# Router logits from unnormalised rows, with the router's transposes and matmuls moved inside the output products

## The reference, cut to what matters

```python
x = x + g1 * y                                  # y = o @ wo, the attention's output product
h2 = _modulate(_rmsnorm(x, norm2_g[i]), sh2, sc2)     # rmsnorm(x) * g * (1 + sc2) + sh2
...
p_grp = softmax((h @ w_r1) + b_r1);  grp = argmax(p_grp)           # h is h2, all tokens
logits2 = einsum('nd,gde->nge', h, w_r2) + b_r2
p_in = softmax(logits2[rows, grp]);  top_p, top_j = lax.top_k(p_in, TOP_K)
...                                             # experts of 1024 -> 2*512 -> 1024, weighted sum
```

## Time and profile before

| what | value |
| --- | --- |
| time, 3 runs | 2983.76 us median (2983.32 to 2985.27) |
| span of the profiled execution, first to last instruction | 2981.8 us |
| median less span | 2.0 us |
| PE busy | 2718.0 us, 91% of the span |
| DVE busy | 1320.2 us, 44% |
| ACT busy | 769.0 us, 26% |
| POOL busy | 607.8 us, 20% |
| mean granted TensorE clock | 0.959 of 2.4 GHz |

### The profile page before, as it was taken

The page is one execution under the profiler, slowest core; times in us unless marked ns, Lnnn a source line. Parts: engine busy times, 40 slices in busy tenths (PEclk is TensorE's granted clock), DMA queues, the critical chain, the costliest instruction groups (busy, mean ns, idle before and its releaser), DMA issues.

```text
span 2981.8 us, 38421 instructions
## 1 busy us (share of the span) xinstructions
PE 2718.0 (91%) x15145; PEld 1490.5 (50%) x15145; DVE 1320.2 (44%) x2419; ACT 769.0 (26%) x1709; POOL 607.8 (20%) x877
## 2 busy tenths in 40 slices
PE   6999999899998996999999969989999869997893
PEld 2444433798897553333333334468884524332331
DVE  3544400799996564111111156479994531110113
ACT  2211100677775101000000034146660100000001
POOL 2555400355554001000000025410000000000000
PEclk9999999999999996999999989989999879999996
DMA  6344468433423227999999864553325479999997
GB/s 251 113 104 141 148 238 280 91 70 77 84 65 116 99 78 299 384 380 426 398 419 396 331 242 141 138 142 65 58 44 205 160 303 417 401 389 397 423 378 291
DMA packets 199410, 684.31 MB, mean 229 GB/s; under 512 B 26688, under 2 KB 122096, under 8 KB 166208
## 3 DMA queue, kind: packets, MB, share of 16 engines
q1 hardware_dynamic: 101344, 583.01, 52.3%
q10 hardware_dynamic: 84896, 61.07, 6.5%
q0 software_dynamic: 12992, 37.77, 3.3%
HBM read 607.81 MB, written 83.43 MB: 232 GB/s over the span
## 4 chain that ended last, share of the span: by engine, by line
PE 78%; DMA 14%; DVE 5%; issue 1%; SPq 1%; ACT 1%; POOL 1%; ACTq 0%; POOLq 0%; DVEq 0%; PEldq 0%
PE psum L461 19%; PE psum L1876 15%; DMA moe_ring<-in_e_w 10%; PE psum L1399 8%; PE psum L1891 8%; PE psum L1048 5%; PE psum L997 5%; PE psum L1186 3%; PE psum L1173 3%; PE psum L1002 2%; PE psum L1214 2%; PE psum L428 1%; PE psum L1388 1%; PE psum L1853 1%; PE psum L2057 1%
## 5 line engine op out<-in xcount | busy, mean ns | idle before, releaser
L1876 PE MATMUL psum<-moe_ring,moe_xT 128*32 128x512 f32 (+2 forms) x3712 | 600.5, 606 | 39.4 <-DMA moe_ring<-in_e_w 37.2
L461 PE MATMUL psum<-qkv_w,act_hT 128*128 128x512 f32 x1376 | 611.8, 598 | 5.5 <-issue 3.1
L461 PEld LDWEIGHTS psum<-qkv_w,act_hT 128*128 128x128 f32 x1376 | 256.4, 191 | 313.3 <-issue 311.2
L1876 PEld LDWEIGHTS psum<-moe_ring,moe_xT 128*32 128x32 f32 (+2 forms) x3712 | 205.7, 123 | 403.2 <-issue 400.4
L1891 PE MATMUL psum<-moe_ring,moe_hT 128*32 128x512 f32 (+2 forms) x1856 | 302.1, 604 | 18.7 <-DMA moe_ring<-in_e_w 17.2
L1960 DVE TENSOR_TENSOR moe_hh<-psum,moe_sg 128x512 f32<-128x512 f32 x42 | 29.0, 691 | 600.0 <-PE psum L1876 600.0
L1399 PE MATMUL psum<-wo,out_oT 128*128 128x512 f32 x576 | 256.1, 599 | 1.9 <-DVEq L1456 1.5
L1928 ACT ACTIVATE moe_sg<-psum 128x512 f32<-128x512 f32 x42 | 25.1, 597 | 749.1 <-PE psum L1876 749.1
L1113 DVE TENSOR_REDUCE att_nmax<-psum 128x1 f32<-128x1280 f32 x144 | 201.8, 1401 | 25.1 <-PE psum L997 23.1
L997 PE MATMUL psum<-att_kT,att_q 128*128 128x512 f32 (+1 forms) x832 | 193.5, 367 | 9.7 <-ACTq L177 5.1
L1065 ACT ACTIVATE att_prob<-psum,att_nmax 128x1280 f32<-128x1280 f32 (+1 forms) x160 | 184.9, 1158 | 48.5 <-DVE att_nmax L1113 45.6
(11 more groups left out here) (263 smaller groups left out, 3294.7 us busy)
## 6 DMA issues: line engine op xcount, KB each, us to landing
moe_ring<-in_e_w SPq DMA_DIRECT2D x192, 2048.0 KB, 20.7
ada_w<-in_ada_w SPq DMA_DIRECT2D x48, 1024.0 KB, 6.5
qk_d<-qkv_stg ACTq DMA_DIRECT2D x112, 256.0 KB, 2.8
att_q<-qk_d SPq DMA_DIRECT2D x32, 640.0 KB, 11.9
att_q<-qk_d SPq DMA_DIRECT2D x64, 256.0 KB, 5.3
qkv_w<-in_a_wqkv SPq DMA_DIRECT2D x6, 2048.0 KB, 10.2
att_kT<-qk_d SPq DMA_DIRECT2D x32, 320.0 KB, 5.7
prep_y<-y_d SPq DMA_DIRECT2D x10, 1024.0 KB, 7.8
```

The source lines that it names most:

```text
L461: ins = nc.tensor.matmul(psum[:, u.par, :], hT[:, k, u.t * P:(u.t + 1) * P], qw[:, u.C % 2, k], start=(k == 0), stop=(k == KD - 1))
L1876: ins = nc.tensor.matmul(psum[part, bank, :], xT[:, 4 * half + k, part], ring[:, slot_of(CHUNK[l][r, half]), k, bank * DE:(bank + 1) * DE] ...
```

## The change

The logits are made from the rows x1 as they are, before the norm. Since h2 = x1 * rs * (gain * (1 + scale)) + shift, with rs one number for a row, the logits are rs * (x1 @ W') + (shift @ W + b), with W' = W whose rows are multiplied by gain * (1 + scale). W' and shift @ W are made once for each layer and each kind of token. For them SP issues three more loads behind the four of the rows, which bring scale, shift and gain as columns: `rcol[p, k]` is element 128k + p, so a load moves 1024 single numbers. That makes six loads in layer 0 and three in layer 1. DVE makes W' and the shifted weights, and PE sums the latter over the partitions with a matrix of ones (`shift_sums`).

The order also changes. PE's transposes of the last tile's x1 stand in the middle of the first half of the product, its `route` behind that half, and `shift_sums` is at that place in the first tile; after the last tile only one `turn` and one `route` are left. DVE does everything for a tile within its own step, and in the last tile makes h2's second operation after the pick. ACT's `lower` waits for h2 before it issues its store. ACT no longer waits for the stores: SP does before expert weights (layer 1) or before its later loads (layer 0), and POOL does before the first gather.

```diff
 def sp_post, step
+                for n, src in enumerate([mod_d[l, t, 4 * D:5 * D], mod_d[l, t, 3 * D:4 * D], norm2_g[l]]):
+                    sp.dma_start(rcol[:, t, n], src.rearrange("(k p) -> p k", p=P), allow_slow_non_contiguous=True).then_inc(s_rcol, 16)
 def pe_post
         def turn(T, par):
-            pe.wait_ge(s_h2, T + 1)
+            pe.wait_ge(s_x1, T + 3)
...
+        def shift_sums():
+            for s in range(2 - l):
+                pe.wait_ge(s_wrs, 2 * l + s + 1)
+                nc.tensor.matmul(psum[:, 6, s * (NG + NE):(s + 1) * (NG + NE)], ones[:, :], wshsum[:, s], start=True, stop=True).then_inc(s_rsh, 1)
...
                 for k in range(KD):
+                    if n == 0 and t and k == KD // 2:
+                        turn(T - 1, 1 - par)
                     ins = nc.tensor.matmul(psum[:, 2 * par + n, :], (oT1 if l else oT)[:, k, t * P:(t + 1) * P], wo[:, k, n * HALF:(n + 1) * HALF], start=(k == 0), stop=(k == KD - 1))
-                if n == 0 and not first:
-                    route(T - 2, par)
+                if n == 0:
+                    if t:
+                        route(t - 1, 1 - par)
+                    else:
+                        shift_sums()
             ins.then_inc(s_y, 1)
-            if not (first and t == 0):
-                turn(T - 1, 1 - par)
...
-        route(T - 2, 0)
         turn(T - 1, 1)
-        route(T - 1, 1)
+        route(TILES[l] - 1, 1)
 def dve_post
+        def router_weights(s):
+            dve.wait_ge(s_rcol, 96 + 48 * l)
+            dvec.link(dve, nc.vector.scalar_tensor_tensor(rcol[:, s, 0], rcol[:, s, 0], 1.0, rcol[:, s, 2], ALU.add, ALU.mult))
+            nc.vector.tensor_tensor(wrs[:, s], wrt[:, l], col_of(0), ALU.mult)
+            dvec.link(dve, nc.vector.tensor_tensor(wsh[:, s], wrt[:, l], col_of(1), ALU.mult))
+            nc.vector.reduce_sum(wshsum[:, s], wsh[:, s].rearrange("p k n -> p n k"), AX).then_inc(s_wrs, 1)
...
+            scaled(T, par, s)
+            if not last:
+                shifted(T, par, s)
+            logit(T, t, par, s)
+            ins = dve_pick(dve, l, t)
+            if last:
+                shifted(T, par, s)
+                ins.then_inc(s_rtp, 1)
...
+        for s in range(2 - l):
+            router_weights(s)
+        for s in range(2 - l):
+            router_bias(s)
+        tile_steps(dve, TILES[l], step)
 def act_post
+            act.wait_ge(s_h2, T + 1)
             act.dma_start(h2_d[ds(t * P, P), :], h2[:, par]).then_inc(s_h2st[par], 16)
...
-        for s in s_x1st + s_h2st:
-            act.wait_ge(s, 16 + 16 * (TA // 2 if l == 0 else (TA + TX) // 2))
 def sp_moe_first (layer 1) and sp_moe (layer 0)
+            for s in s_x1st + s_h2st:
+                sp.wait_ge(s, post_stored(l))
 def pool_moe
+        for s in s_h2st:
+            pool.wait_ge(s, post_stored(l))
```

More of the change, by code:

```diff
@@ L1307, in build @@
     s_bc, s_bcd = [sem("s_bc0"), sem("s_bc1")], sem("s_bcd")
+    s_rcol, s_wrs, s_rsh, s_rbias = sem("s_rcol"), sem("s_wrs"), sem("s_rsh"), sem("s_rbias")
     A = Arena("post")
@@ L1340, in build @@
     bc1 = A("bc1", [P, 1, 4, D])
+    rcol = A("rcol", [P, 2, 3, KD])
+    wrs = A("wrs", [P, 2, KD, NG + NE])
+    wsh = A("wsh", [P, 2, KD, NG + NE])
+    wshsum = A("wshsum", [P, 2, NG + NE])
+    rbias = A("rbias", [P, 2, NG + NE])
     BC, XT = [bc, bc1], [xt, xt1]
@@ L1379, in turn, with route @@
             for k in range(KD):
-                ins = nc.tensor.transpose(psum[:, 4 + k // 4, (k % 4) * P:(k % 4 + 1) * P], h2[:, par, k * P:(k + 1) * P], ident)
+                ins = nc.tensor.transpose(psum[:, 4 + k // 4, (k % 4) * P:(k % 4 + 1) * P], x1[:, par, k * P:(k + 1) * P], ident)
             ins.then_inc(s_h2t, 1)
-        def route(T, par):
+        def shift_sums():
+            for s in range(2 - l):
+                pe.wait_ge(s_wrs, 2 * l + s + 1)
+                nc.tensor.matmul(psum[:, 6, s * (NG + NE):(s + 1) * (NG + NE)], ones[:, :], wshsum[:, s], start=True, stop=True).then_inc(s_rsh, 1)
+        def route(t, par):
+            T = TA * l + t
+            s = int(t >= TX)
             pe.wait_ge(s_h2ta, T + 2)
@@ L1386, in route @@
             pe.wait_ge(s_rld, T + 1)
+            if t == 0:
+                pe.wait_ge(s_rbias, 2 + l)
             for k in range(KD):
-                ins = nc.tensor.matmul(psum[:, 6 + par, 0:NG + NE], h2T[:, par, k, :], wrt[:, l, k, :], start=(k == 0), stop=(k == KD - 1))
+                ins = nc.tensor.matmul(psum[:, 6 + par, 0:NG + NE], h2T[:, par, k, :], wrs[:, s, k, :], start=(k == 0), stop=(k == KD - 1))
             ins.then_inc(s_rl, 1)
@@ L1460, in dve_post, with router_bias @@
             dve_fixed(dve)
+        def router_weights(s):
+            col_of = lambda n: rcol[:, s, n].unsqueeze(2).broadcast_to([P, KD, NG + NE])
+            dve.wait_ge(s_rcol, 96 + 48 * l)
[3 more added lines that the diff above has]
+            nc.vector.reduce_sum(wshsum[:, s], wsh[:, s].rearrange("p k n -> p n k"), AX).then_inc(s_wrs, 1)
+        def router_bias(s):
+            dve.wait_ge(s_rsh, 2 + l)
+            nc.vector.tensor_tensor(rbias[:, s], psum[:, 6, s * (NG + NE):(s + 1) * (NG + NE)], brt[:, l, :], ALU.add).then_inc(s_rbias, 1)
         def upper(T, par):
@@ L1465, in upper, with scaled, shifted, logit @@
             nc.vector.tensor_copy(h2T[:, par, 4:8, :], psum[:, 5, :].rearrange("p (b n) -> p b n", b=4)).then_inc(s_h2td, 1)
-        def logit(t, par):
-            T = TA * l + t
+        def scaled(T, par, s):
+            dve.wait_ge(s_x1rs, T + 1)
+            nc.vector.scalar_tensor_tensor(hm[:, par], x1[:, par], xrs[:, par:par + 1], BC[l][:, s, 2], ALU.mult, ALU.mult).then_inc(s_h, 1)
+        def shifted(T, par, s):
+            dve.wait_ge(s_h, T + 1)
+            dve.wait_ge(s_h2st[par], 8 * (T - par + 2))
+            nc.vector.tensor_tensor(h2[:, par], hm[:, par], BC[l][:, s, 1], ALU.add).then_inc(s_h2, 1)
+        def logit(T, t, par, s):
             dve.wait_ge(s_rl, T + 1)
-            nc.vector.tensor_tensor(logits[:, ds(t, 1), :].rearrange("p o n -> p (o n)"), psum[:, 6 + par, 0:NG + NE], brt[:, l, :], ALU.add).then_inc(s_rld, 1)
+            dve.wait_ge(s_rbias, 2 * l + s + 1)
+            nc.vector.scalar_tensor_tensor(logits[:, t, :], psum[:, 6 + par, 0:NG + NE], xrs[:, par:par + 1], rbias[:, s], ALU.mult, ALU.add).then_inc(s_rld, 1)
+            dve.wait_ge(s_rld, T + 3)
         def step(t, par):
             T = TA * l + t
-            s = int(isinstance(t, int) and t >= TX)
-            begin = isinstance(t, int) and t in (0, TX)
+            s = int(t >= TX)
+            begin = t in (0, TX)
             if begin:
@@ L1487, in step @@
             dve.sem_inc(s_pinfree, 1)
-            later = not (isinstance(t, int) and t == 0)
-            if later:
-                upper(T - 1, 1 - par)
+            upper(T, par)
             if begin:
                 dve.wait_ge(s_bcd, 1 + s + 2 * l)
[L1493 to L1505, removed]
+            last = t == TILES[l] - 1
+            scaled(T, par, s)
[6 more added lines that the diff above has]
+                ins.then_inc(s_rtp, 1)
+            else:
+                dvec.link(dve, ins)
+        for s in range(2 - l):
[3 more added lines that the diff above has]
+        tile_steps(dve, TILES[l], step)
     def act_post(act, l):
@@ L1511, in act_post, with lower @@
             act.sem_inc(s_h2ta, 1)
-        def lower(t, par, whole=False):
+        def lower(t, par):
             T = TA * l + t
@@ L1528, in step @@
             act.dma_start(xs_d[ds(t * P, P), :], x1[:, par]).then_inc(s_x1st[par], 16)
-            if not (isinstance(t, int) and t == 0):
-                lower(t - 1, 1 - par)
+            lower(t, par)
         tile_steps(act, TILES[l], step)
-        lower(TILES[l] - 1, 1, True)
-        for s in s_x1st + s_h2st:
-            act.wait_ge(s, 16 + 16 * (TA // 2 if l == 0 else (TA + TX) // 2))
     def pool_post(pool, l):
@@ L1797, in sp_moe_loads, with post_stored @@
                 sp.dma_start(ring[:, slot_of(n)].rearrange("p k f -> p (k f)"), src.rearrange("p o k f -> p (o k f)")).then_inc(s_ring[slot_of(n)], 16)
+    def post_stored(l):
+        return 16 + 16 * (TA // 2 if l == 0 else (TA + TX) // 2)
     def sp_moe_first(sp, l):
+        if l:
+            for s in s_x1st + s_h2st:
+                sp.wait_ge(s, post_stored(l))
         sp.wait_ge(s_exptab, l + 1)
@@ L1804, in sp_moe @@
     def sp_moe(sp, l):
+        if l == 0:
+            for s in s_x1st + s_h2st:
+                sp.wait_ge(s, post_stored(l))
         sp.wait_ge(s_xg[0], xg_count(l, 0))
```

5 lines of the change are left out of this document (1 added, 4 removed).

## The result

The changed kernel takes 3006.78 us (median of 4 runs, 3004.87 to 3011.47) against 2983.54 for the one before (4 runs, 2977.60 to 2985.27). That is 23.2 us slower, where 3002 us was forecast. The measured ratio is 1.0086, with a 95% interval of 1.0073 to 1.0098; the two medians alone give 1.0078. The profiled execution has a span of 3004.3 us, 22.5 more than before.

What follows compares the result with a forecast made beforehand. PE alone was taken to limit post's loop. 16.9 + 10.0 + 3.4 + 1.0 - 5.0 - 8.2 = +18.1 us on the 2981.8 span, plus 2.0 to the median, gave 3002 us; range 2988 to 3009, eight in ten 2991 to 3017.

Steps and rivals of the forecast that it cites:

- PE's wait: First tile of post: PE idles for the columns before its second half product, clock loss included; +16.9 us layer 0, +10.0 layer 1.
- the clock's share: After PE's idle stretch in the first tile the clock is at half for 5 us; 2.5 us lost in each layer.
- Why the columns are late: Start of post: column loads queue behind the rows on SP, 0.7 us each, six 4.2, landing at 974.5 in layer 0.
- One of its signs of being wrong: Column loads in post: the prediction is wrong if one takes more than 1.5 us of the queue.
- 2.0 us for each transfer: Column loads: if each paid about 2.0 us in turn, six would be 12 us and the sum rise by about 11.7.
- Rival 1: Column loads of single numbers cost 2.7 us each in the queue; nine at 2.0 more make +18, 3020 us; chance 0.15.
- Rival 2: PE's turns inside the products wait for x1; half a us for each of 16 is +8, 3010 us; chance 0.05.
- Rival 3: Columns pass the rows at post's start, PE idles 4.3 and about 1.1 us; -0.9, 2983 us, no change; chance 0.08.
- Rival 4: PE doesn't wait for the columns at all in the first tile; -8.8, 2975 us; chance 0.05.
- The loop: Post's tile loop: one route per layer moves in from the tail at 1.7 us each, +3.4 us over both layers.
- The tail: End of post: gate opens 14.05 us after the last y, -5.0 us in layer 0 and -8.2 in layer 1.
- The gather: Start of moe, layer 1: delayed expert loads overlap the first gather; +1.0 us, between 0 and 1.4.

Runs made afterwards that it cites:

- e2_runs_first: Changed kernel with column loads as 128 runs of 32 bytes, issued ahead of the first x and the rows: 2981.20 us, ratio 0.9990 to the kernel before.
- e4_late_sums: Changed kernel, column loads unchanged, but DVE makes the weights behind the first x1 and PE sums the shifts in the second tile: 2982.21 us, ratio 0.9996.
- e6_loads_only: Kernel before plus the nine column loads of single numbers at their place in SP's order, their data unused: 2982.26 us, ratio 1.0000.
- e7_warm_stall: Changed kernel with 13 (layer 0) and 6 (layer 1) matmuls nobody reads ahead of PE's wait for the weights: 3000.18 us, ratio 1.0059.
- e10_runs16_look: Kernel before plus nine loads of 1024 runs of 16 bytes into a spare tile, at the column loads' place: one run, 2987.03 us.
- e1_runs32: Changed kernel with the width split the other way, so a column load is 128 runs of 32 bytes, same order: 2998.09 us, ratio 1.0046.
- e11_numbers_first: Changed kernel with its column loads of single numbers issued by SP ahead of x and the rows: one run, 2981.24 us.
- e5_act_queue: Changed kernel with its column loads of single numbers issued by ACT at the start of post, instead of SP: 3021.22 us, ratio 1.0132.
- e3_stores_only: Kernel before with only the waits for the stores moved from ACT to SP and POOL: 2980.07 us, ratio 0.9990.

## Why the prediction was right, point by point

**PE's wait** (16.9 and 10.0 forecast). Measured 17.4 and 9.65 from the first y's. It is shown to be the loss by e2_runs_first and e4_late_sums, which remove it in two ways and both end level with the kernel before, and by e6_loads_only, where the loads without the wait cost nothing. PE went on 15.0 us (979.60) and 6.6 us (2271.95) behind the end of its first half product, the sums' own products included as they were in the forecast's 14.4 and 7.5; the clock's share was 2.2 and 2.9 for 2.5 each (e7_warm_stall). In layer 0 the first y of kernels that share the old order lies anywhere from 15.51 (e6_loads_only) to 17.07 us (e10_runs16_look) behind the start of the product, which begins at the lower clock in all of them; so the 17.4 is known to about a microsecond.

**Why the columns are late.** The prediction had them behind the rows in one queue at 0.7 us each. That much holds: in either group of layer 0 the third column landed within 1.5 us of the row ahead of it. But it missed that SP itself is held, 2.9 to 3.6 us for each load after the first of a group, so that the second rows left 8 us later. The landing time came out right (974.5 forecast, 975.8 measured, with the stage starting 0.6 later) because two errors offset each other, which was luck: the last row, issued at 966.16, landed 8.2 us later, at 974.3 and not at 970.3, and the last three columns needed 1.4 us behind it, where 4.2 had been set for six. The row landed so soon after its late issue because, as it seems, less stood ahead of it. In e1_runs32, where SP isn't held, the first y comes 5.3 and 2.1 us earlier: that is 7.4 of the 27.0 us of loss, which the 1024 runs account for and the forecast had no term for. One of its signs of being wrong, a column load that takes more than 1.5 us of the queue, was met as a hold of SP and not as time in the stream of transfers. What holds the issue isn't settled. e11_numbers_first excludes a fixed time for making 1024 runs, e10_runs16_look the size of a run; that the queue has room for so many runs only would fit both, and wasn't tried by itself.

The prediction also set 2.0 us for each transfer against its 0.7. In the section that it names, that figure is a fit for transfers that GpSimd issues; here, on SP's queue, the six columns of e11_numbers_first were all there 5.9 us after the first issue (955.58 to 961.47), where six turns of 2.0 would be 12.

**Rivals.** Rival 1 (dear loads) is refuted as a price of the transfer: six of 2.7 us would be 16, and e11_numbers_first has them there in 5.9. As a hold of SP it was nearer than the forecast. Rival 2 (turns that wait for x1) is refuted too: the loop's tiles are 16.4 us apart, 147.66 for nine. Rival 3 (the columns pass the rows) is refuted by the changed kernel itself, and on a queue of their own in e5_act_queue they didn't pass either. Rival 4 (no wait) isn't what happened, and its 2975 is contradicted by e2_runs_first: without any wait the new router gives 2981.

**The loop: the step that was mis-sized.** The prediction charged one route per layer, 1.7 us. From first to last y it is 147.66 for 145.00 and 114.88 for 112.23: 2.7 in each layer. The missing 0.9 is a turn. Before, the turn of the last tile but one stood behind the last product, beside x1 on DVE, where it cost nothing; now it stands inside. In all 5.3 for 3.4.

**The tail** (-5.0 and -8.2 forecast). Measured -4.8 and -7.9, the gate 14.38 behind y and not 14.05. The gate waits for ACT's issue of the store, which starts at 1150.46, and opens 0.58 us later. Of layer 1's gain, 3.1 belong to the stores' wait alone (e3_stores_only).

**The gather** (+1.0 forecast). The gather itself took 1.8 us more in layer 1 and 0.4 in layer 0. Waits of SP's queue in the changed kernel, layer 1:

```profile
SPq L1847 <- DMA h_d<-postb_h: 20.4, 1, 20.4
```

SP waited for the last store, which needed 8.0 us, and issued its three expert loads 8.4 us behind the gate (2419.60) instead of 4.8. So they ran into the gather for longer than forecast. But that layer 1's slower gather reaches the end isn't shown, and the profiles speak against it. From layer 1's gate to the first expert product the thirteen profiles have 28.3 to 32.1 us. From that gate to the end of the kernel the seven with a slow gather (over 29 us) have 593.2 us on average, and the six with a fast one (under 28.5) have 593.2 too; the changed kernel has 593.1, the one before 594.3. Behind the first product PE waits again and again for expert weights, whose loads take about a third of the chain there, and they, as it seems, take the gather's loss back.

**The sum.** Up to the gates, and with 0.5 for layer 0 between its gate and its first expert product, it is 17.4 + 9.65 + 5.3 - 4.8 - 7.9 + 0.5 = 20.2 us; 18.1 were forecast, with the gather. The span grew by 22.5. The rest lies in stretches that the change doesn't touch: the start of post came 0.6 later, from layer 0's first expert product to post of layer 1 it was 3.0 more, and from layer 1's gate to the end 1.3 less. Over all profiles here the second of these varies from 1071.0 to 1075.4 us, so a single profile carries some us of scatter that no edit explains.

## What to carry to other kernels

A tiny load is as late as what stands ahead of it in its queue, so the first thing that an engine will wait for must be issued first; the same nine loads cost 27 us behind the rows and about 1 us ahead of them, and giving them a queue of their own beside 6 MB of other traffic made it worse. Before work is moved from a stage's tail into its full loop, count which pieces of the tail were already covered; here the reordering paid 5.3 us inside to gain some 9.6 outside, and 5.8 of those could be had in the old order by filling PE's idle time with matmuls that nobody reads.

## What the runs showed of the hardware that wasn't expected

Behind 2.6 MB of x and rows, loads of 1024 runs held SP's queue for 2.9 to 3.6 us each after the first of a group, with 4 or 16 bytes a run alike; issued ahead of x and rows, they took 0.4 to 0.7 us each. On a second queue beside 2-MB loads the last such load took 26.3 us to land. The clock could be held in the tail by eight records, 3.60 us in all, behind the last product: the route behind them took 1.98 us for 3.63.
